# Two chained transformer blocks on one core: projections with 512 weight columns moving over 128 stationary tokens

## The chip, the core and the metric

The kernel runs on one core of a Trainium2 chip. The metric is the device time of one launch in microseconds; the median of three runs is compared. Inputs and output lie in the chip's memory in float32; all weights (about 277 MB) are read once per launch.

## The reference, cut to what matters

256 tokens of width 1024 pass through two models of two layers each, one after the other. Each layer has a mixer and one or two feed-forward blocks of width 2816, six of them in all; two have a causal convolution of three taps on the gate:

```python
def conv_ffn(h, w_up, conv_w, conv_b, w_down):          # blocks 0 and 1
    u, g = jnp.split(h @ w_up, 2, axis=-1)
    g = causal_dwconv(g, conv_w, conv_b)
    return (jax.nn.silu(g) * u) @ w_down
def _swiglu(x, wg, wu, wd):                             # blocks 2 to 5
    return (jax.nn.silu(x @ wg) * (x @ wu)) @ wd
# first model:  x = x + f(rmsnorm(x)), a final rmsnorm at its end
# second model: x = x + s * rmsnorm(f(rmsnorm(x)))      # s = 0.5 or 1, a norm on the output too
```

The mixers, in order: an mLSTM with four heads of 192 ("a") beside attention to 256 memory tokens; attention in a band with a relative bias ("band", 12 heads) beside memory attention; a convolution module of 31 taps on 512 channels beside windowed attention ("swa", 8 heads); attention with forget gates ("fox", 16 heads). Each has an input projection from width 1024 and an output projection back to it.

## The kernel before

It is written engine by engine, with semaphores by hand. Matrix products run in float32r with each operand as a rounded high part and the rest: `three` (L1571) issues hi x hi, hi x lo and lo x hi. Every product of weights is thus three matmuls.

**Weights.** They come in 260 slots of 1 MB, SLOTW = 8 x 256 columns per partition, a ring of RING = 3. SyncE's `load` (L407) waits for lo_done of the slot three before and issues one DMA into raw. ScalarE's `split_hi` (L587) rounds raw into w_hi once PE has used that slot three before (w_used), VectorE's `split_lo` (L950) subtracts into w_lo. raw, w_hi and w_lo are three separate rings.

**Form.** x is kept with its features on the partitions (xT, 8 chunks of 128 by 256 tokens). `feature_major` (L1604) holds 128x128 blocks of weights stationary and moves 256 tokens:

```python
for m in range(widths):
    for k in range(NCH):
        ins = three(bank[:, m * SEQ:(m + 1) * SEQ], weights(base, k * COLS + m * P), source(k),
                    start=k == 0, stop=k == NCH - 1)
```

`token_major` (L1615), for values, holds 128 tokens stationary and moves the 256 columns of a slot; it is the smaller part. `down` (L1627) adds the two hidden chunks of a step into the eight chunks of the output, which stay in four banks acc.

**Feed-forward.** `ffn` exists on each engine (SyncE L429, ScalarE L638, VectorE L1018, PE L1688). A block has 11 steps of three slots (gate, up, down) of 48 matmuls each. PE runs, in a hardware loop, gate and up of step i and then down of step i-1, so the elementwise work of a step is beneath the next one's products. Gate and up are scaled by the norm's factor as they are taken from the banks (L1030, L1048), silu is ScalarE's (L662), the product L1054, its two parts L666 and L1058; with the convolution, L655 and L1039 add the taps.

**Norms.** ScalarE applies the gain to x (`apply_hi`, L610) and squares it; the sum over features crosses partitions, so PE does it: `light_mean` (L1656: L1659, L1660) on sums made by VectorE (L982, L983), and `square_mean` (L1640: 32 matmuls of one column at L1645, then L1652 to spread the factor) for the norms on outputs. `token_rstd` (L1662, L1666) brings the factor to the tokens' side. `first_slot` (L1670: L1677, L1678, L1682) orders the first slot's products by what is ready. `post` (L1001) updates x (L1007, L1008). Clears of acc are matmuls with zeros (L1698).

**Order around mixers.** `slot` and `project` (L1848, L1726) interleave projections with attention stages `scores`, `turns` (transposing the probabilities, L1800) and `values`. The 31 taps of two convolution channels are diagonal matmuls (L1984), those of the other two VectorE's (L1460). `narrow` (L1832) makes gate logits of 8 and 16 columns. At the end the output is transposed back (L2060) and stored.

## Time and profile before

| | us |
|---|---|
| median of 3 runs | 1859.78 |
| lowest and highest | 1851.17, 1880.07 |
| the profiled execution: span, first to last instruction | 1852.6 |

Of the profiled execution the span is what is shown; it lies between the lowest and the median run. Durations below come from it. A matmul's recorded length reaches into its successors, since matmuls are pipelined; what one costs in a dense stretch is the distance between two starts. Line numbers are those of the kernel above.

### The profile page before, as it was taken

Reading aid. Unit: us, or ns where it says so; the run is one execution under the profiler, and the core shown is the slowest. Engines: PE = TensorE matmul, PEld = TensorE weight load, DVE = VectorE, ACT = ScalarE, POOL = GpSimd, SP = SyncE. Lnnn points to the kernel's source line nnn. Section 1 sums busy time; section 2 is a strip of 40 time slices with the busy share of each in tenths; the row PEclk is TensorE's granted clock in tenths of the full one; section 3 lists DMA queues with packets and bytes.
Section 4 is the critical chain, followed back from the end, with each engine's and each line's share of the span. In section 5 each row is a group of like instructions: output and inputs, shape, how many; then the busy total and the mean of one; then the engine's idle time right before and its main releaser. Section 6 shows DMA issues by size and latency. Waiting matters only on the chain.

```text
span 1852.6 us, 33184 instructions
## 1 busy us (share of the span) xinstructions
PE 1768.5 (95%) x13819; PEld 1699.4 (92%) x13825; DVE 1124.6 (61%) x1411; ACT 806.7 (44%) x950; POOL 85.2 (5%) x120
## 2 busy tenths in 40 slices
PE   7998999999899999999998799998999899999998
PEld 7996999998599999999997789998999898889997
DVE  5864766675466666555578475556655644475554
ACT  4543544443454444433442553335434433444332
POOL 3000000000000000000086000000000000000000
PEclk9997999999899999999999899999999979899998
DMA  8441456574045554655522245553655432246551
GB/s 257 137 138 46 154 188 196 185 215 159 1 151 195 191 169 139 199 181 181 181 92 72 83 145 181 181 181 118 200 182 181 136 115 92 68 137 204 181 181 45
DMA packets 226905, 279.62 MB, mean 151 GB/s; under 512 B 6848, under 2 KB 208850, under 8 KB 226840
## 3 DMA queue, kind: packets, MB, share of 16 engines
q1 hardware_dynamic: 226200, 278.41, 46.6%
q8 instruction: 47, 0.77, 0.2%
q0 software_dynamic: 640, 0.29, 0.1%
q14 instruction: 18, 0.15, 0.0%
HBM read 277.48 MB, written 1.07 MB: 150 GB/s over the span
## 4 chain that ended last, share of the span: by engine, by line
PE 88%; DVE 8%; ACT 2%; DMA 1%; issue 1%; DVEq 0%; SPq 0%; ACTq 0%
PE two L1573 26%; PE two L1575 26%; PE two L1574 26%; PE two L1776 2%; PE two L1645 1%; DVE aux L1460 1%; DVE act_lo L972 1%; PE two L1800 1%; DVE xT L1008 1%; DVE qk L1007 1%; PE two L1782 1%; PE two L1926 1%; DMA raw<-in_w_kv 1%; PE two L1811 1%; PE two L1787 1%
## 5 line engine op out<-in xcount | busy, mean ns | idle before, releaser
L1573 PE MATMUL two<-act_hi,w_hi 128*128 128x256 f32 x2648 | 759.3, 287 | 11.7 <-DVE act_lo L1168 6.8
L1574 PE MATMUL two<-act_lo,w_hi 128*128 128x256 f32 x2648 | 754.4, 285 | 0.0
L1575 PE MATMUL two<-act_hi,w_lo 128*128 128x256 f32 x2648 | 754.4, 285 | 0.0
L956 DVE TENSOR_TENSOR w_lo<-raw,w_hi 128x2048 fp32r<-128x2048 f32 x260 | 595.7, 2291 | 251.9 <-ACT w_hi L596 251.3
L596 ACT CAST w_hi<-raw 128x2048 fp32r<-128x2048 f32 x260 | 494.9, 1903 | 375.2 <-PE two L1575 194.0
L1573 PEld LDWEIGHTS two<-act_hi,w_hi 128*128 128x128 f32 x2648 | 513.6, 194 | 15.2 <-DVE act_lo L1168 7.8
L1574 PEld LDWEIGHTS two<-act_lo,w_hi 128*128 128x128 f32 x2648 | 513.7, 194 | 0.3
L1575 PEld LDWEIGHTS two<-act_hi,w_lo 128*128 128x128 f32 x2648 | 513.4, 194 | 0.0
L1573 PE MATMUL two<-hid_hi,w_hi 128*128 128x256 f32 x1072 | 302.2, 282 | 8.6 <-DVE hid_lo L1058 8.6
L1575 PE MATMUL two<-hid_hi,w_lo 128*128 128x256 f32 x1072 | 301.6, 281 | 0.0
L1574 PE MATMUL two<-hid_lo,w_hi 128*128 128x256 f32 x1072 | 298.9, 279 | 0.0
L1573 PEld LDWEIGHTS two<-hid_hi,w_hi 128*128 128x128 f32 x1072 | 202.4, 189 | 9.8 <-DVE hid_lo L1058 9.8
L1574 PEld LDWEIGHTS two<-hid_lo,w_hi 128*128 128x128 f32 x1072 | 202.4, 189 | 0.0
L1575 PEld LDWEIGHTS two<-hid_hi,w_lo 128*128 128x128 f32 x1072 | 201.8, 188 | 0.0
L666 ACT CAST hid_hi<-work 128x512 fp32r<-128x512 f32 x66 | 40.9, 620 | 233.5 <-PE two L1575 222.8
L1058 DVE TENSOR_TENSOR hid_lo<-work,hid_hi 128x512 fp32r<-128x512 f32 x66 | 45.7, 692 | 121.7 <-ACT hid_hi L666 121.7
L1030 DVE TENSOR_TENSOR work<-two,rstd 128x512 f32<-128x512 f32 x66 | 45.6, 691 | 54.4 <-PE two L1575 54.1
L1677 PE MATMUL two<-act_hi,w_hi 128*128 128x256 f32 x176 | 49.7, 314 | 13.9 <-ACT act_hi L617 13.8
L655 ACT ACTIVATE work<-work,par 128x256 f32<-128x256 f32 x44 | 24.1, 595 | 89.4 <-DVE work L1030 89.4
L1573 PE MATMUL two<-w_hi,act_hi 128*128 128x256 f32 (+1 forms) x208 | 62.0, 298 | 0.0
L1574 PE MATMUL two<-w_lo,act_hi 128*128 128x256 f32 (+1 forms) x208 | 61.1, 294 | 0.0
L1575 PE MATMUL two<-w_hi,act_lo 128*128 128x256 f32 (+1 forms) x208 | 60.9, 293 | 0.0
(273 smaller groups left out, 1696.7 us busy)
## 6 DMA issues: line engine op xcount, KB each, us to landing
raw<-in_ffn_w_up SPq DMA_DIRECT2D x88, 1024.0 KB, 5.2
raw<-in_ffn_w_down SPq DMA_DIRECT2D x66, 1024.0 KB, 4.9
raw<-in_ffn_w_gate SPq DMA_DIRECT2D x44, 1024.0 KB, 5.3
raw<-in_a_w_in SPq DMA_DIRECT2D x13, 1024.0 KB, 5.2
raw<-in_fox_w_in SPq DMA_DIRECT2D x12, 1024.0 KB, 5.3
raw<-in_ab_w_in SPq DMA_DIRECT2D x7, 1024.0 KB, 5.3
raw<-in_w_kv SPq DMA_DIRECT2D x6, 1024.0 KB, 6.6
raw<-in_mem_w_kv SPq DMA_DIRECT2D x4, 1024.0 KB, 10.0
```

Source lines behind the costliest of these rows:

```text
L596: nc.scalar.copy(w_hi[:, r, :], raw[:, r, :]).then_inc(hi_done, 1)
L655: ins = nc.scalar.activation(gate_cv[:, j, :], gate_acc[:, j, :], ACT.Identity, bias=bb, scale=w2)
L666: nc.scalar.copy(hid_hi[:, :, :], hid[:, :, :]).then_inc(ff_hi, 1)
L956: nc.vector.tensor_tensor(w_lo[:, r, :], raw[:, r, :], w_hi[:, r, :], ALU.subtract).then_inc(lo_done, 1)
L972: nc.vector.scalar_tensor_tensor(out=act_lo[:, c, :], in0=xT[:, c, :], scalar=cols(col, c), in1=act_hi[:, c, :], op0=ALU.mult, op1=ALU.sub ...
L1030: nc.vector.tensor_tensor(gate_acc[:, :, :], pj[t % RING][:, :].rearrange("p (j t) -> p j t", j=2), rstd2, ALU.mult).then_inc(ff_raw, 1)
L1058: nc.vector.tensor_tensor(hid_lo[:, :, :], hid[:, :, :], hid_hi[:, :, :], ALU.subtract).then_inc(ff_lo, 1)
L1573: nc.tensor.matmul(dst, w[0], a[0], start=start, stop=False, skip_group_check=True)
L1574: nc.tensor.matmul(dst, w[0], a[1], start=False, stop=False, skip_group_check=True)
L1575: return nc.tensor.matmul(dst, w[1], a[0], start=False, stop=stop, skip_group_check=True)
L1677: nc.tensor.matmul(d, w[0], act_hi[:, k, :], start=k == 0 and m == 0, stop=False, skip_group_check=True)
L1776: ins = nc.tensor.matmul(dst[:, lo:hi], q[:, b * P:(b + 1) * P], k[:, 0:hi - lo], start=True, stop=kind not in ("fox", "band"), skip_group ...
```

## The change

Almost every function is rewritten. What it does:

- **Form.** In every projection the activations of 128 tokens (a block b, of two) are stationary, and 512 weight columns move. A group is 1024 x 512 weights: `project(name, b)` runs 24 matmuls for block 0 and, later, 24 for block 1. Gate and up of a step share a group (256 columns each); down and the output projections move 512 of the 1024 output columns.
- **Tokens.** x is kept with tokens on the partitions (x_tok). What needs features on the partitions is transposed by PE: x before each norm (16 of 128x128, `turn_x`), the hidden values (2 per block and step, 4 with the convolution), q, k, gates and keys (`turn`). Row sums come from ScalarE's accum_out, so the statistics on PE, `narrow` and the clears go; gate logits are columns of a group of 264.
- **Slots.** 520 slots of half a megabyte in a ring of 10. raw and w_lo are the same memory, so a slot is loaded again only when PE is done with the slot ten before (FREED). Gate and up come as two DMAs per slot. ScalarE and VectorE split up to a given slot at given places (`splits`).
- **Out of step.** Block 0 is finished before block 1 in the last step and in the output projections, so that its norm can start. The loops of the feed-forward blocks are written out.
- **Mixers.** band: the last two pairs' stages lie in the output projection. fox: pairs 0 to 2 between projections, 3 to 7 after them, one at a time. swa: 26 of VectorE's 62 taps before the keys are taken.

Its core, with the rest left out (in this order: buffers, SyncE's waits, the order of ScalarE in a block, `arrive` between blocks, ScalarE's and VectorE's part of a step without the convolution, PE's `project` and its feed-forward block; VectorE's order is ScalarE's):

```diff
-COLS = 256
-RING = 3
-SLOTW = NCH * COLS
+HALF = 512
+RING = 10
+SLOTE = 1056
...
-        raw = sb("raw", [P, RING, SLOTW])
-        w_hi = sb("w_hi", [P, RING, SLOTW], F32R)
-        w_lo = sb("w_lo", [P, RING, SLOTW], F32R)
-        xT = sb("xT", [P, NCH, SEQ])
+        w_hi = sb("w_hi", [P, RING, SLOTE], F32R)
+        with nc.sbuf_tensor("raw", [P, RING, SLOTE], F32) as raw:
+            pass
+        w_lo = sb("w_lo", [P, RING, SLOTE], F32R)
+        x_tok = sb("x_tok", [P, NTB, D])
...
+            def slot_free(t):
+                if t < RING:
+                    return
+                kind, n = FREED[t - RING]
+                sp.wait_ge({"tm": w_tm, "pj": pj_full[1], "dn": w_dn, "acc": acc_full}[kind], n)
...
+                for s in range(2, LAST):
+                    go(s, 0)
+                    splits(first + 6 * s + 7)
+                    out_of(s, 0)
+                    splits(first + 6 * s + 9)
+                    go(s, 1)
+                    splits(first + 6 * s + 11)
+                    out_of(s, 1)
+                    splits(first + 6 * s + 13)
...
+            def arrive(e, key, table):
+                first = OUT[EVENTS[e]][0] + NCH if EVENTS[e] in OUT else FFN_AT[EVENTS[e]] + 6 * STEPS
+                ni = NORMS[key][2]
+                fetch_table(ACT.Sqrt)
+                for b in range(NTB):
+                    if e >= POST:
+                        moment_h(e, b)
+                    if e == FINAL:
+                        moment_x(N_FINAL, b)
+                    if b:
+                        moment_x(ni, 0)
+                    normed_hi(key, b)
+                    if b == 0:
+                        splits(first + 3)
+                moment_x(ni, 1)
+                splits(first + 5)
...
+                def silu(s, b):
+                    nc.scalar.activation(gate_t[b], pj[b][:, 0:FW], ACT.Silu, scale=rx[:, b:b + 1]).then_inc(ff_ga[b], 1)
...
+                def gated(s, b):
+                    nc.vector.scalar_tensor_tensor(out=hid_t[b], in0=pj[b][:, FW:2 * FW], scalar=rx[:, b:b + 1], in1=gate_t[b],
+                                                   op0=ALU.mult, op1=ALU.mult).then_inc(pj_free[b], 1)
...
+            def project(name, b):
+                a, ns, n = GROUPS[name]
+                per = NCH // ns
+                if GI[name]:
+                    pe.wait_ge(pj_free[b], GI[name])
+                for k in range(NCH):
+                    t = a + k // per
+                    if k % per == 0:
+                        slot_ready(t)
+                    hi, lo = whole_slot(t, per)
+                    mm(pj[b][:, 0:n], act_part(0, k, b), hi[:, k % per, :], k == 0, False)
+                    mm(pj[b][:, 0:n], act_part(0, k, b), lo[:, k % per, :], False, False)
+                    ins = mm(pj[b][:, 0:n], act_part(1, k, b), hi[:, k % per, :], False, k == NCH - 1)
...
+                for s in range(2, LAST):
+                    project((f, s), 0)
+                    down(s - 1, 1, (0, 1))
+                    turn_hid(s, 0)
+                    project((f, s), 1)
+                    down(s, 0, (0, 1))
+                    turn_hid(s, 1)
+                project((f, LAST), 0)
+                down(LAST - 1, 1, (0,))
+                turn_hid(LAST, 0)
+                project((f, LAST), 1)
+                down(LAST, 0, (0,))
+                turn_hid(LAST, 1)
+                down(LAST, 0, (1,))
+                down(LAST - 1, 1, (1,))
+                down(LAST, 1, (0, 1))
```

With the convolution, `take` (ScalarE) brings gate and up out of the bank, PE turns all four chunks, and `conv_hid` runs over ScalarE and VectorE by turns: copy into a padded buffer, six operations on 128 columns (one per tap and chunk), silu, product, high part, low part.

## Rows read from the trace of the kernel before

**Rows 1.** The page: its first line, part 1, and PEclk of part 2

```profile
span 1852.6 us, 33184 instructions
PE 1768.5 (95%) x13819; PEld 1699.4 (92%) x13825; DVE 1124.6 (61%) x1411; ACT 806.7 (44%) x950; POOL 85.2 (5%) x120
...
PEclk9997999999899999999999899999999979899998
```

**Rows 2.** The page, part 4: the chain that ended last, by engine

```profile
PE 88%; DVE 8%; ACT 2%; DMA 1%; issue 1%; DVEq 0%; SPq 0%; ACTq 0%
```

**Rows 3.** Stretches: PE, PEld, DVE, ACT, POOL busy us, PEclk, DMA share, GB/s

```profile
588.82:605.99 17.17, 17.17 (x147) 17.17 (x145) 11.18 (x12) 7.87 (x7) 0.00 (x0) 1.00 0.54 183
...
1332.00:1349.17 17.17, 17.17 (x146) 17.17 (x145) 9.65 (x7) 6.77 (x5) 0.00 (x0) 1.00 0.58 183
1250.29:1297.65 47.36, 41.71 (x333) 39.84 (x333) 32.66 (x42) 25.02 (x31) 0.00 (x0) 1.00 0.39 123
...
1835.00:1852.60 17.60, 10.89 (x73) 9.16 (x71) 8.04 (x15) 4.07 (x8) 0.00 (x0) 0.73 0.16 60
```

**Rows 4.** PE in order of time: start us, us; feed-forward, narrow, half clock

```profile
1320.25 0.28 PE L1574 MATMUL two<-hid_lo,w_hi 128*128 128x256 f32 x1
1320.37 0.28 PE L1575 MATMUL two<-hid_hi,w_lo 128*128 128x256 f32 x1
...
80.53 0.25 PE L1575 MATMUL two<-gw_hi,act_lo 128*128 128x8 f32 x1
80.64 0.25 PE L1573 MATMUL two<-gw_hi,act_hi 128*128 128x8 f32 x1
...
1473.02 0.41 PE L1677 MATMUL two<-act_hi,w_hi 128*128 128x256 f32 x1
1473.23 0.41 PE L1678 MATMUL two<-act_hi,w_lo 128*128 128x256 f32 x1
```

**Rows 5.** L1984 alone in 10 us: PE and PEld busy, PEclk, DMA

```profile
978.00:988.00 10.00, 10.00 (x48) 8.73 (x47) 1.00 0.94 296
```

**Rows 6.** PE by line: form, count | busy us, mean ns | idle before

```profile
L1645 PE MATMUL two<-mean_w,nrm 128*128 128x1 f32 x224 | 26.3, 245 | 0.2 <-ACT nrm L636 0.2
L1800 PE MATMUL two<-ident,p_sb 128*128 128x128 f32 x140 | 22.6, 307 | 17.6 <-DVE p_sb L1161 17.6
...
L1659 PE MATMUL two<-nrm,mean_w 128*128 128x256 f32 x20 | 7.0, 431 | 6.2 <-DVE nrm L983 6.1
...
L1698 PE MATMUL two<-zero 128*128 128x512 bf16 x18 | 5.5, 422 | 0.5 <-issue 0.2
```

**Rows 7.** In order of time, PE, a turn of eight

```profile
493.50 1.09 PE L1800 MATMUL two<-ident,p_sb 128*128 128x128 f32 x8 [2.27 <-DVE p_sb L1161]
```

**Rows 8.** VectorE and ScalarE by line: form, count | busy us, mean ns

```profile
L1039 DVE SCALAR_TENSOR_TENSOR work<-work,par 128x255 f32<-128x255 f32 x44 | 19.4, 481 | 32.8 <-ACT work L655 32.8
...
L982 DVE TENSOR_TENSOR nrm<-nrm 128x1024 f32<-128x1024 f32 x10 | 12.3, 1230 | 5.4 <-ACT nrm L622 5.4
...
L1161 DVE TENSOR_SCALAR p_sb<-p_sb,small 128x128 f32<-128x128 f32 x36 | 10.2, 284 | 0.6
...
L596 ACT CAST w_hi<-raw 128x2048 fp32r<-128x2048 f32 x260 | 494.9, 1903 | 375.2 <-PE two L1575 194.0
...
L666 ACT CAST hid_hi<-work 128x512 fp32r<-128x512 f32 x66 | 40.9, 620 | 233.5 <-PE two L1575 222.8
```

**Rows 9.** The page, part 6: KB each, us from issue to landing

```profile
raw<-in_ffn_w_gate SPq DMA_DIRECT2D x44, 1024.0 KB, 5.3
...
out_x<-qk SPq DMA_DIRECT2D x4, 256.0 KB, 2.0
```

**Rows 10.** In order of time, PE: turns of two successive pairs of band

```profile
472.62 0.82 PE L1800 MATMUL two<-ident,p_sb 128*128 128x128 f32 x6
...
478.25 0.82 PE L1800 MATMUL two<-ident,p_sb 128*128 128x128 f32 x6
```

**Rows 11.** The chain in order of time: VectorE's taps in the swa mixer

```profile
978.33 16.65 DVE aux L1460 x41
```

More of the change, by code:

```diff
@@ L685, in projection @@
-            def projection(first, n, take=None, after=None, ahead=()):
-                for t in range(first, first + n):
-                    if t - first not in ahead:
-                        split_hi(t + 2)
-                    if take:
-                        take(t, t - first)
-                    if after and t - first in after:
-                        after[t - first]()
-            def out_projection(first):
-                for j in range(4):
-                    split_hi(first + j + 2)
-                    post_squares(j, first + 3, None)
+            split = [0]
@@ L760, in _ @@
[L760 to L774 removed]
+            act.wait_ge(ident_ready, 1)
@@ new lines, in _ @@
+            for j in range(3):
+                for b in range(NTB):
+                    take_kv(j, b)
+                    if j == 2:
+                        normed_hi("band", b)
+                    splits(GROUPS[f"KV{j}"][0] + 9 + 2 * b)
+            for j in range(2):
+                for b in range(NTB):
+                    to_tk(f"BIN{j}", "band", b).then_inc(pj_free[b], 1)
+                    splits(GROUPS[f"BIN{j}"][0] + 9 + 2 * b)
+            attention("band", lambda n: splits(137) if n == 1 else None)
@@ new lines, in _ @@
+            exps("fox", 1)
+            take_pair(2, 1)
+            o_hi("fox", 0)
+            pt_copy("fox", 1)
+            take_pair(3, 0)
+            o_hi("fox", 1)
+            exps("fox", 2)
+            take_pair(3, 1)
+            pt_copy("fox", 2)
+            for n in range(3, 8):
+                exps("fox", n)
+                o_hi("fox", n - 1)
+                pt_copy("fox", n)
+            o_hi("fox", 7)
+            splits(459)
+            arrive(EV["fox"], 5, ACT.Silu)
+            ffn(5, False)
@@ L939, in _ @@
+            fetch_table(ACT.Sqrt)
+            for b in range(NTB):
+                moment_h(EV[5], b)
         @block.vector
@@ L1569, in _ @@
+            o_lo("fox", 7)
+            splits(459)
+            arrive(EV["fox"], 5)
+            ffn(5, False)
+            for b in range(NTB):
+                residual(EV[5], b)
         @block.tensor
         def _(pe):
[L1571 to L1575 removed]
@@ new lines, in _ @@
+            for b in range(NTB):
+                pe.wait_ge(al, 8 * b + 8)
+                project("M0", b)
+            pe.wait_ge(params_in, 16 * 16)
+            for n in range(PARAM_TILES):
+                ins = nc.tensor.transpose(acc[1][n // 4][:, n % 4 * P:(n % 4 + 1) * P], prow[:, n, :], ident[:, :])
+                if n in (3, 4):
+                    ins.then_inc(par_ps, 1)
+            turn("M0", 0, 2)
+            project("M1", 0)
+            turn("M0", 1, 2)
+            turn_x("a", 0)
@@ new lines, in attention_start, with pair_ready @@
+            def attention_start(phase):
+                last = len(PAIRS[phase])
+                for n in range(last):
+                    scores(phase, n)
+                    if n >= 1:
+                        turns(phase, n - 1)
+                    if n >= 2:
+                        values(phase, n - 2)
+            def pair_ready(phase, first):
+                return lambda c, b: pe.wait_ge(h_olo, PAIR0[phase] + c - first + 1)
+            attention_start("band")
+            pe.wait_ge(h_olo, PAIR0["band"] + 6)
@@ new lines, in _ @@
+            scores("fox", 0)
+            project("FP2", 0)
+            turn("FP1", 1, 4)
+            turns("fox", 0)
+            scores("fox", 1)
+            project("FP2", 1)
+            turn("FP2", 0, 4)
+            values("fox", 0)
+            turns("fox", 1)
+            project("FP3", 0)
+            turn("FP2", 1, 4)
+            values("fox", 1)
+            scores("fox", 2)
+            project("FP3", 1)
+            turn("FP3", 0, 4)
+            turns("fox", 2)
+            scores("fox", 3)
@@ new lines, in _, with last_turns, last_values @@
+            turn("FP3", 1, 4)
+            values("fox", 2)
+            all_taken("FP3", "FP3")
+            for n in range(3, 7):
+                turns("fox", n)
+                scores("fox", n + 1)
+                values("fox", n)
+            pe.wait_ge(h_olo, PAIR0["fox"] + 6)
+            def last_turns():
+                turns("fox", 7)
+            def last_values():
+                values("fox", 7)
+            project_out("fox", pair_ready("fox", 0), {1: last_turns, 3: last_values})
```

2179 lines of the change are left out of this document (1140 added, 1039 removed).

## The prediction

> **What bounds the kernel now.** I read the page from its top. TensorE is busy 95% of the span, VectorE 61%, ScalarE 44%, and the strip of 40 slices shows PE at 9 nearly everywhere at a granted clock of 0.9 to 1.0 [rows 1]. A busy PE need not be one that sets the end, so the chain of waits comes next: 88% of it is PE, 8% DVE, 1% DMA [rows 2]. Then the six feed-forward blocks by stretch: a step of one takes 17.17 us, with the convolution or without, PE busy in all of it, VectorE 9.6 to 11.2, ScalarE 6.8 to 7.9, at full clock [rows 3]. A step has three slots of 48 matmuls, 144, so one costs 17.17/144 = 119.2 ns. There are 260 slots: 12,480 such matmuls, 1488 us of 1852.6. The rest (365 us) is attention, convolution, mLSTM, statistics and what PE waits. So the price of one matmul is the question.
>
> **What one matmul costs.** All are 128x128 weights under 256 moving columns, and start 120 ns apart (the last of a feed-forward slot 120 or less) [rows 4]. Two rows bracket what that is. The narrow products with only 8 moving columns still start 110 ns apart (80.53, 80.64): that is the weight load's pace. And where the granted clock was 0.5 (1.2 GHz), the same 256-column form starts 213 ns apart, 256/1.2, with a new weight block each time: with 213 ns of streaming the load is hidden whole [rows 4]. The taps L1984 say the same at full clock: 10 us hold 48 of them, one or two of which are cut by the edges, so they start 208 to 217 ns apart, each with its own weights [rows 5]. At full clock the 256 columns themselves would need 107 ns, less than the load, so today the load sets the pace and the columns are nearly free.
>
> **Part 1, 512 columns over one load.** The columns in all stay the same and the loads halve. New count: 87 groups of 48 with 512 columns (4176), 66 down steps of 24 (1584), four output projections of 96 (384), 6144 in all, and four narrow groups (256 or 264 columns) of 48, 192. The form isn't in the trace. Its floor is 213 ns (a column per cycle at 2.4 GHz, from the 213 at half that clock), its ceiling two of today's, 238. I take 216, the 213 of streaming and a little, which lies in L1984's 208 to 217. Then 6144 x 0.216 + 192 x 0.12 = 1350 us against 1488: **-138**. At 213 it is -156, at 238 -3.
>
> **Part 2, tokens on the partitions need turning.** Added transpositions of 128x128: hidden values 4 per plain step and 8 per step with convolution (352), x ten times 16 less today's 16 (144), q, k, gates and keys 114, less the 16 at the end: 594. Eight of L1800 take 1.09 us, one 0.31, so (1.09-0.31)/7 = 0.11 apart [rows 7]: **+65**. Bounds: 0.11, and 0.307 if each took its whole length (+182). In the Trainium skill, "TensorE: Matmul & The Clock Gate", Part 4 (PE-mode transpose), such a transposition took about 275 ns in one kernel's context; by it the sum here would be 163 us instead of 65. The trace disagrees for groups of them, which is how the change issues them; I stay with the row.
>
> **Part 3, statistics leave PE.** Row sums come from ScalarE's accumulator. Gone: L1645 (26.3 us), L1659 and its twin L1660 (7.0 and somewhat less, 13), L1652 and L1666 (44 at 0.11: 5), the narrow products (96 x 0.11, partly at half clock: 14), the clears L1698 (5.5) [rows 6]: **-64**. Parts 1 to 3 are all on PE and so on the path: -138 +65 -64 = -137.
>
> **Part 4, does a step keep up?** A plain step on PE: 72 x 0.216 + 4 x 0.11 = 16.0 us; with convolution 16.4. Splitting half a megabyte: ScalarE between 620 ns (512 columns, L666) and 1903 (2048, L596), by the line through them 1.05 us; VectorE 1.23 (L982 has that size) [rows 8]. Six of each are 6.3 and 7.4 us, plus some 2 each for silu, products and parts: no bound. What can bind is the order. raw and w_lo are now one buffer, so a load waits for PE's last use ten slots before, no longer for the split three slots before. Call the start of project(s, 0) zero. Slots 6s+8 and 6s+9 come free at 7.1 and 7.8, in down(s-1, 1). 1 MB lands in 5.3 us and 256 KB in 2.0 [rows 9]; the second of two half-megabytes so lands about 5.2 after the first's issue, at 12.5. Cast 13.6, silu(s, 1) 14.1 (its project ended at 13.2), VectorE's split 14.8, gated product 15.3; turn_hid(s, 1) is due at 15.7. It holds by 0.4 us. All other slots have over 3 us. With the convolution ScalarE and VectorE pass the block to and fro five times. For block 0 that is about 4.6 us beneath 5.2 of matmuls. For block 1 the splits of 6s+10 and 6s+11 stand before it on VectorE, conv_hid starts some 1.5 us late (six operations of 128 columns, between the 284 ns of L1161 and the 440 of L1039: about 2 us), and down(s, 1) waits about 1 us. Queued behind it are hi and lo of the next slots, which have slack. I take 1.0 us x 22 steps: **+22** (bounds 0 and 2 per step). SP issues 10 loads a step at 0.37 us where it had 3; it waits for slots most of the time, so nothing. The loops are written out, so code is fetched where it was repeated; straight stretches today run at the same 120 ns: nothing.
>
> **Part 5, the joints.** From the last steady step to the first of the next block takes 47.36 us where two steps take 34.34 [rows 3]: 13.0 for a joint with a norm on the output, of which 5 are PE's statistics (32 L1645 at 0.11, a few more). After: block 0's sums and update (squares of 512 columns as L666, 0.6 twice, small ones, two updates on VectorE of 0.7, between L1039 and L982: about 4.2 us) lie under 3.9 us of block 1's down products; then 16 turns (1.8). But ScalarE does normed_hi of block 0 and two splits (4.5 us) before block 1's squares, so PE runs dry after block 0's first 16 products, about 4 us. 1.8+0.5+4 = 6.3. For six such joints -6.5 each; statistics and turns of these are in parts 2 and 3, so what is new here is small: the idle time stays about as it was. I take 0. The end: 17.6 us from the statistics to the last store, with four transposed stores; about 7 after, of it -4 not counted yet.
>
> **Part 6, the rest.** Memory keys start when half a megabyte is there: -6. band: the last two pairs of eight lie under the output projection; a pair comes every 5.63 us [rows 10]: -5. swa: the taps stood alone on the chain for 16.65 us [rows 11]; 26 of 62 now lie beneath projections: -10. fox: pairs 3 to 7 come after the projections one at a time (about 9 us each, half of it PE), where only two did: +7. Sum: -18, with the end.
>
> **Sum.** -137 +22 +0 -18 = -133: 1852.6 - 133 = 1720 us by the profiled span, which has nothing beside it but the start of the launch. The median of the runs shown is 1859.8, 0.4% above it, so 1720 x 1.004 = **1726 us**.
>
> **Rivals.** (A) The 120 ns are 107 of streaming plus 13 of changing weights, whatever the width: 226 ns, 6144 x 0.010 = +61, **1787**. For it: 120 is above both the load's pace and the streaming. Against: 213 at half clock and 217 at L1984 leave no room. (B, the slower side) **The slot chain sets the step.** If the second half-megabyte lands later than 5.6 us after the first's issue, turn_hid(s, 1) waits, every wait delays the slots' release, and nothing catches up; the two engines' strict order adds the convolution's. The gate and up slots are two loads each of 256 KB; if none overlapped, eight at 2.0 us and two at 3.1 would make a step of 22 us, and midway between that and my 16.3 lies 19.2: 66 x 2.9 = +191, **1917**. It decides against the change once the mean step is over 18.3, 2.0 above mine. For it: 0.4 us of slack, and three times as many loads. Against: the DMA engines are 0.55 busy in a step [rows 3], and a late block has slack elsewhere. A weaker form (0.7 us a step) gives 1772. (C) Each turn takes its whole 0.307, as a mean L1800 does [rows 6], where it stands between other matmuls: 594 x 0.20 = +119, **1845**. For it: here they come in twos and fours, not eights. Against: nothing waits between them. The figure of the Trainium skill's Part 4 above points the same way. (D) No stall in the convolution and block 1's joint hidden: -22 -15, **1689**. (E) The new order hides nothing and the form costs 238: +135, 1861; the rows on 213 and 217 leave it almost nothing.
>
> **How the numbers follow.** Chances: forecast 0.54, A 0.10, B 0.06, its weak form 0.13, C 0.04, D 0.12, E 0.01. Forecast 1726; the range takes in D's, A's and the weak B's spread, from 1665 to 1800. This kernel's measurement tells about 2% from no change, so the bounds are 1823 and 1897 us: faster takes the forecast, D, the weak form and nearly all of A, 0.87; same takes C, E and the edges, 0.08; slower is what of B exceeds 2% and unforeseen waits of that kind, 0.05.
>
> **What would show it.** Right: in the timeline w_hi matmuls of 512 columns start 215 to 217 ns apart (A: 226; E: 238); a plain step lasts 16.0 us, one with convolution 17.4; transpositions 0.11 apart; PE's idle time before its turns of hidden values and its down products about 1 us per convolution step and next to none in a plain one; in the joints one wait of about 4 us before the second turning of x. Wrong: idle time of PE released by w_lo in the middle of blocks (B), or a granted clock that falls in the joints.

## The result and the profile after

The changed kernel takes 1914.47 us (median of 4 runs, 1909.69 to 1915.55) against 1869.92 of the runs of before beside it; without the disturbed ones the ratio is 1.031, 95% interval 1.028 to 1.034. It is 3% slower where 7% faster was forecast. The profiled execution has a span of 1913.8, 61.2 more than before's 1852.6. Its page, the rows that answer to [rows 1, 2] (first line, part 1, PEclk of part 2, engines of part 4) and three groups of part 5:

```profile
span 1913.8 us, 20929 instructions
PE 1770.6 (93%) x7823; PEld 1393.0 (73%) x7823; DVE 1059.2 (55%) x1848; ACT 934.2 (49%) x1599; POOL 82.3 (4%) x128
...
PEclk9997999999799999999998899999999998589999
...
PE 71%; DVE 11%; DMA 7%; ACT 6%; SPq 3%; issue 1%; DVEq 0%; ACTq 0%
...
L1704 PE MATMUL two<-w_hi,act_parts 128*128 128x512 f32 (+2 forms) x3120 | 1021.2, 400 | 38.0 <-DVE w_lo L1138 24.3
...
L647 ACT CAST w_hi<-raw 128x1024 fp32r<-128x1024 f32 (+1 forms) x520 | 533.9, 1053 | 203.4 <-DMA raw<-in_ffn_w_up 159.2
```

Two things stand in it. PE's matmuls are nearly halved in number (7823 records for 13819), yet PE is busy for the same time, 1770.6 us for 1768.5. And the chain is no longer PE's alone: 71% for 88%, the rest VectorE, DMA, ScalarE and SyncE's queue, so waits of another kind have come. ScalarE's casts now wait 159 us for loads of w_up; that alone would cost nothing, if the casts were early enough.

The strip shows one new place, a 5 in slice 35 of PEclk (1627 to 1675 us), in the fox mixer.

Stretches of after (us, then PE, PEld, DVE, ACT, POOL busy, PEclk, DMA share, GB/s): a plain step, a later plain step, one with convolution, step 3 of the first block, and fox's pairs after the last projection. Before had 17.17 for every step [rows 3].

```profile
1172.76:1189.81 17.05, 17.05 (x78) 13.86 (x77) 8.89 (x10) 7.82 (x10) 0.00 (x0) 1.00 0.55 185
1189.81:1207.78 17.97, 17.27 (x78) 13.79 (x77) 8.87 (x10) 7.79 (x10) 0.00 (x0) 1.00 0.54 175
628.17:645.94 17.77, 17.77 (x81) 14.23 (x80) 12.54 (x22) 9.47 (x14) 0.00 (x0) 1.00 0.54 178
246.12:269.33 23.21, 18.15 (x81) 14.01 (x80) 12.01 (x22) 9.76 (x14) 1.41 (x2) 1.00 0.95 280
...
1625.00:1690.00 65.00, 50.94 (x161) 32.51 (x162) 17.99 (x84) 14.59 (x50) 0.00 (x0) 0.50 0.02 6
```

A plain step in which PE never waits takes 17.05 us, not the 16.0 of the forecast: that is the form's price. The next one takes 0.9 more and PE is busy for 0.7 less than the stretch: that is a wait. The form's pace is seen in order of time (PE, start us, us); the starts lie 0.22 to 0.24 apart, where [rows 4] had 0.12 for half the columns:

```profile
1175.75 0.39 PE L1704 MATMUL two<-w_hi,act_parts 128*128 128x512 f32 x1
1175.98 0.39 PE L1704 MATMUL two<-w_lo,act_parts 128*128 128x512 f32 x1
1176.21 0.62 PE L1704 MATMUL two<-w_hi,act_parts 128*128 128x512 f32 x2
1176.66 0.39 PE L1704 MATMUL two<-w_lo,act_parts 128*128 128x512 f32 x1
```

**A ledger of PE.** All of PE's intervals from one start to the next, added up by what started them; what goes beyond 245 ns (512 weight columns), 135 (fewer weight columns, and the sums L1645, L1659, L1660), 115 (the new turnings) or 700 (all else) is counted as waiting. So the last row also has some products that ran at half clock, and the attention row some short waits.

```
us                                     before    after   difference   forecast
products of weights                    1497.8   1447.6      -50        -138
turnings to the features' side            1.7     56.3      +55         +65
statistics on PE, with the clears        56.1      0        -56         -64
products of attention and the rest      179.3    211.2      +32        }  +4
waiting                                 108.2    188.7      +80        }
sum                                      1843     1904      +61        -133
```

The miss is 194 us: 88 in the pace of the products, 108 in waits and in attention and the rest, 8 in the statistics, and 10 the other way in the turnings. The experiments take the first two in turn.

One stage has over half of the 61 us. From its first products to those of the next stage the fox mixer takes 170.4 us before and 204.9 after, at a mean granted clock of 0.87 and 0.77 (before from L1677 to L1677, after from one turning of x to the next):

```profile
1472.50:1642.90 170.40, 167.23 (x1111) 149.26 (x1113) 86.13 (x192) 67.33 (x123) 0.00 (x0) 0.87 0.31 100
...
1507.30:1712.20 204.90, 175.04 (x729) 131.80 (x728) 83.67 (x212) 82.51 (x170) 0.53 (x1) 0.77 0.29 96
```

### The profile page after: what moved, and what is told of

It is laid out like the page before. It is cut to its first block, busy times and chain, and to the rows that moved or that the text cites. A ratio compares the mean times of both kernels' runs of the same rounds, so it can differ in the third digit from the quotient of the medians.

```text
span 1913.8 us, 20929 instructions
## 1 busy us (share of the span) xinstructions
PE 1770.6 (93%) x7823; PEld 1393.0 (73%) x7823; DVE 1059.2 (55%) x1848; ACT 934.2 (49%) x1599; POOL 82.3 (4%) x128
## 4 chain that ended last, share of the span: by engine, by line
PE 71%; DVE 11%; DMA 7%; ACT 6%; SPq 3%; issue 1%; DVEq 0%; ACTq 0%
PE two L1704 59%; DMA raw<-in_ffn_w_up 6%; DVE w_lo L1138 4%; ACT w_hi L647 3%; PE two L1762 2%; PE two L1895 2%; DMA raw<-in_ffn_w_down 2%; SPq L451 1%; PE two L1918 1%; PE two L2143 1%; PE two L1900 1%; SPq L452 1%; ACT act_parts L686 1%; PE two L1776 1%; DVE act_parts L1155 1%
## 5 line engine op out<-in xcount | busy, mean ns | idle before, releaser
L1704 PE MATMUL two<-w_hi,act_parts 128*128 128x512 f32 (+2 forms) x3120 | 1021.2, 400 | 38.0 <-DVE w_lo L1138 24.3
L1138 DVE TENSOR_TENSOR w_lo<-raw,w_hi 128x1024 fp32r<-128x1024 f32 (+1 forms) x520 | 623.5, 1223 | 265.8 <-ACT w_hi L647 261.4
L1704 PEld LDWEIGHTS two<-w_hi,act_parts 128*128 128x128 f32 x3120 | 593.3, 192 | 173.6 <-DVE w_lo L1138 27.1
L647 ACT CAST w_hi<-raw 128x1024 fp32r<-128x1024 f32 (+1 forms) x520 | 533.9, 1053 | 203.4 <-DMA raw<-in_ffn_w_up 159.2
L1704 PE MATMUL two<-w_lo,act_parts 128*128 128x512 f32 (+1 forms) x1560 | 612.0, 393 | 0.0
L1704 PE MATMUL two<-w_hi,hid_parts 128*128 128x512 f32 x1008 | 337.9, 396 | 5.6 <-DVE hid_parts L1244 5.4
L1704 PEld LDWEIGHTS two<-w_lo,act_parts 128*128 128x128 f32 x1560 | 300.3, 192 | 58.4
L1704 PEld LDWEIGHTS two<-w_hi,hid_parts 128*128 128x128 f32 x1008 | 189.4, 188 | 54.8 <-DVE hid_parts L1244 11.8
L1704 PE MATMUL two<-w_lo,hid_parts 128*128 128x512 f32 x504 | 198.1, 393 | 0.0
L1704 PEld LDWEIGHTS two<-w_lo,hid_parts 128*128 128x128 f32 x504 | 94.7, 188 | 21.1
L724 ACT ACTIVATE p_sb<-two,rx 128x256 f32<-128x256 f32 x88 | 41.6, 472 | 117.4 <-PE two L1704 117.4
```

What stands on the lines that cost most here:

```text
L647: nc.scalar.copy(w_hi[:, t % RING, 0:n], raw[:, t % RING, 0:n]).then_inc(hi_done, 1)
L724: nc.scalar.activation(gate_t[b], pj[b][:, 0:FW], ACT.Silu, scale=rx[:, b:b + 1]).then_inc(ff_ga[b], 1)
L1138: nc.vector.tensor_tensor(w_lo[:, r, 0:n], raw[:, r, 0:n], w_hi[:, r, 0:n], ALU.subtract).then_inc(lo_done, 1)
L1704: return nc.tensor.matmul(dst, a, w, start=start, stop=stop, skip_group_check=True)
```

## Experiments on the price of the form

**forms.** Matmuls alone, 96 of a form in a row, on tiles made ready before (float32r if not said otherwise).

```diff
+            run(512)      # 2 the form of the change
+            run(256)      # 3
+            run(384)      # 4
+            run(128)      # 5
+            run(512, wide=64)      # 11 64 stationary columns
+            run(512, rows=64)      # 12
+            mm(bank[3][:, 0:SEQ], plain[:, 0:P], plain[:, 256:512], i == 0, i == 23)      # 13 plain float32
```

> A kernel of matmuls alone, 96 of each form in a row, copies x to the output and computes nothing of the reference. It measures what one matmul costs from start to start at full clock. Rows of the two traces: 256 columns 120 ns, 512 columns 231 ns; at half clock 213 and 426, so nothing beside the streaming there. Theory F (a fixed price for changing weights, none of it hidden): 384 columns 160+13 to 18 = 173 to 178 ns, 512 with 64 stationary columns the same 231, one weight block repeated 231. Theory L (the load of the next weights takes reads from the stream of 4-byte columns): 64 stationary columns about 222, 64 rows the same 231, bf16 213 at 512 columns since load and stream are half as large. Theory B (VectorE and ScalarE disturb the reads): 213 to 216 here with both idle, 231 only in the last group, where both are busy. My theory is L at 0.6, F at 0.3, B at 0.1. All: 128 columns 108 to 110.

Median interval between two starts of a group, and what is left when a column per cycle at 2.4 GHz is taken off:

```
128 columns              111 ns      -        bf16, 256 columns       109 ns    2
256                      120        13        bf16, 512               216       3
384                      173        13        64 stationary columns   230      17
512                      227        14        64 rows                 227      14
256 tokens over weights  120        13        plain float32, 256      216 and 213, two records each
```

Five stretches of it (10 us of 256 columns, of 512, of bf16 512, of 64 stationary columns, and of 512 beside busy VectorE and ScalarE; a window's count has one or two cut at its edges), at a granted clock of 1.00, the upper level:

```profile
58.00:68.00 10.00, 10.00 (x86) 10.00 (x85) 0.00 (x0) 0.00 (x0) 0.00 (x0) 1.00 0.01 2
...
110.00:120.00 10.00, 10.00 (x46) 8.29 (x45) 0.00 (x0) 0.00 (x0) 0.00 (x0) 1.00 0.00 0
152.00:162.00 10.00, 10.00 (x47) 4.55 (x47) 0.00 (x0) 0.00 (x0) 0.00 (x0) 1.00 0.00 0
...
184.00:194.00 10.00, 10.00 (x45) 5.85 (x44) 0.00 (x0) 0.00 (x0) 0.00 (x0) 1.00 0.01 2
...
258.00:268.00 10.00, 10.00 (x46) 8.29 (x45) 4.85 (x9) 2.92 (x6) 0.00 (x0) 1.00 0.00 0
```

The 13 ns are fixed: the same at 256, 384 and 512 columns, whichever operand is held. That is rival A of the prediction, which I had given 0.10. My own theory of this experiment fell: 64 stationary columns, whose load is shorter (5.85/44 = 133 ns for 184), save nothing. One weight block repeated, four banks in turn and busy neighbours change nothing either (227 each). bf16 pays 3 ns, which agrees with the formula of the Trainium skill, "TensorE: Matmul & The Clock Gate", Part 2 (back-to-back issue gap): N/2.4 GHz and about 2.5 ns. The 131 ns at 512 columns which the same section gives for a sustained stream is not what these rows show (216). The float32r form pays some 10 ns more than bf16. The cause inside PE stays open. Plain float32 shows where the forecast went wrong: its 256 columns are two records of 213 to 216 ns each, so each passes at two cycles of 2.4 GHz per column, and so do the taps of [rows 5] (62 products, 124 records).

**halves.** The kernel after with each product of 512 columns as two of 256. Both halves of a first product carry the start flag into one bank, and the output is not the reference's; the products and columns that pass through PE are those of a correct split.

```diff
+                if n == 512:
+                    nc.tensor.matmul(dst[:, 0:256], a, w[:, 0:256], start=start, ...)
+                    return nc.tensor.matmul(dst[:, 256:512], a, w[:, 256:512], start=start, ...)
```

> The kernel after with each matmul of 512 columns issued as two of 256 over the same tokens; everything else stays. It gives what the wide form is worth in this kernel. If the wide form costs 231 and the narrow one 120, 6144 x 9 ns = 55 us more than after, 1970 us less what idle time absorbs (some 90 us of waits, of which those for PE's own work stay): 1955 to 1970. If the wide form were free streaming at 213 (the forecast), the narrow would cost 150 us more, 2065. If the slots and not PE set the time of a step (rival B of the prediction), nothing changes: 1914 to 1925.

1945.45 us, ratio 1.052 (1.045 to 1.059) to before: 2.1% over after's 1.031, some 39 us, and less than the 1955 to 1970 expected. A pair of halves takes 239.2 ns on average from start to start, the whole 230.8, so 6144 x 8.4 = 52 us of PE, of which the waits take a part. The wide form is a gain, but of 8 ns, not of 22.

**forms2.** In forms the product takes 227, in after 231, in a pattern (224 to 238) that comes back in every step. This run issues the steps of after without anything else.

```diff
+            for g in range(4):      # 2 slots 1024 apart
+                project(4 * g, 1024, b4[0:2], act)
+            for g in range(4):      # 3 slots 1056 apart, as in the kernel
+                project(4 * g, 1056, b4[0:2], act)
```

> A kernel of matmuls alone that copies x to the output and computes nothing of the reference: the project and down products of the kernel after, 4 steps of each kind. The form alone took 227 ns in the first kernel of matmuls, the kernel after has a mean of 231, in a pattern of 224 to 238 that repeats from step to step whatever VectorE and ScalarE do. Theory A (the place of the slots in memory, 1056 columns apart instead of 1024): 227 with slots 1024 apart, 231 with 1056. Theory W (waits and marks of semaphores): 227 without, 231 with them. Theory T (the products for down and the turns between them): 227 until these come in. If all stay at 227, what PE reads is not the cause, and how it gets its instructions is what is left.

Mean interval: 226.7 ns with slots 1024 columns apart, 230.5 with 1056, 226.9 with 1088; waits, marks, down products and turns add nothing (230.5 to 230.6). 40 us at 1024, at 1056 and at 1088:

```profile
52.00:92.00 40.00, 40.00 (x178) 33.15 (x177) 0.00 (x0) 0.00 (x0) 0.00 (x0) 1.00 0.00 0
96.00:136.00 40.00, 40.00 (x176) 32.57 (x175) 0.00 (x0) 0.00 (x0) 0.00 (x0) 1.00 0.00 0
...
300.00:340.00 40.00, 40.00 (x179) 33.11 (x178) 0.00 (x0) 0.00 (x0) 0.00 (x0) 1.00 0.00 1
```

So the slots' place costs 4 ns per product on average. 1056 columns are 16.5 times 256 bytes, so every other slot starts in the middle of such a block; 1024 and 1088 are whole multiples. Three distances were tried; that the 256 bytes are what counts is read from these alone.

**align.**

```diff
-SLOTE = 1056
+SLOTE = 1088
```

> The kernel after with slots 1088 columns apart (17 x 256 bytes) instead of 1056 (16.5 x 256), one constant. In the second kernel of matmuls slots 1024 or 1088 apart gave 226.8 ns between starts, 1056 gave 230.5. If that is so here, 6144 matmuls become 3.7 ns shorter: 23 us of PE's time; with what the waits take of it 12 to 23 us less than the kernel after on this chip. If the waits for slots are the bound, PE waits longer by what it saves: 0 to 8 us.

1911.17, where the kernel after on the same chip took 1919.01 (**after_again**, below): 8 us, which is within what one kernel moves between chips. The median interval falls to 227, but that into the turnings rises from 374 to 421 ns on average (158 of them): PE waits where it had worked.

**twice.** sched (below) with each turning of hidden values issued twice.

```diff
-                for c in range(n):
+                for c in list(range(n)) * (1 if isinstance(name, str) else 2):
```

> sched with each turning of hidden values issued twice (352 more of 128x128, the second writes what the first wrote); otherwise the result is the same. In sched nothing waits in the steps: 17.03 us plain, 17.51 with convolution. If a turning costs its distance in a dense group (109 ns, part 2 of the prediction), a plain step lasts 17.03 + 4 x 0.109 = 17.47, one with convolution 17.51 + 8 x 0.109 = 18.38, and the whole is 38 us over sched: 1935. If each cost its whole recorded length (0.28, rival C), 18.15 and 19.75 and 98 us more, 1995.

1927.05, 29 us over sched (on another chip). The steps, where nothing else is idle, are exact: a plain one 17.50 for 17.04, one with convolution 18.36 for 17.51.

```profile
1178.57:1196.07 17.50, 17.50 (x82) 14.30 (x81) 8.72 (x11) 7.37 (x10) 0.00 (x0) 1.00 0.54 180
646.64:665.00 18.36, 18.36 (x90) 15.19 (x89) 12.45 (x23) 9.43 (x15) 0.00 (x0) 1.00 0.52 173
```

0.46/4 and 0.85/8: 0.11 us each. Rival C is dead, and part 2 stands. The 275 ns that the Trainium skill's "TensorE: Matmul & The Clock Gate", Part 4 (PE-mode transpose) gives for a transposition is close to the recorded length here (273 ns on average in sched), not what one costs in a group.

## Experiments on the waits

What happens in the slow step of after: the chain in order of time from 1189.30, when PE is done with a slot of down.

```profile
1189.31 0.37 SPq L451
...
1189.72 1.20 SPq L452
...
1190.97 0.47 SPq L451
...
1191.48 4.93 DMA raw<-in_ffn_w_up
...
1196.43 1.06 ACT w_hi L647
...
1197.52 1.22 DVE w_lo L1138
1198.74 0.41 DVE p_sb L1217
...
1199.19 0.44 PE two L1762 x2
```

The block's silu (L724) could start at 1195.9 but stands behind the cast of slot 6s+9 on ScalarE, whose load has just landed; the gated product stands behind the split on VectorE; the turning is 0.70 us late. This is the place and the order of the prediction's part 4, which found 0.4 us of slack: it let 4.7 us pass from the release to the landing, and 7.1 pass (1189.30 to 1196.41), since SyncE's issues take 0.4 to 1.2 us each where four are due at once, and 256 KB land in 4.9, not 2.0. The row of 2.0 was a store's [rows 9]; the loads of 256 KB here take 4.0 to 4.7 by the medians of the page.

**sched.** The splits of 6s+8 and 6s+9 behind block 1's silu and product.

```diff
                     out_of(s, 0)
-                    splits(first + 6 * s + 9)
                     go(s, 1)
-                    splits(first + 6 * s + 11)
+                    splits(first + 6 * s + 9)
                     out_of(s, 1)
-                    splits(first + 6 * s + 13)
+                    splits(first + 6 * s + 11)
```

> The kernel after with ScalarE's and VectorE's splits of slots 6s+8 and 6s+9 behind silu and product of block 1 instead of ahead of them, and the later ones one place later too (in the steps 2 to 9 of a block). In after 158 waits ahead of a turning of hidden values cost 23 us above the pace of the products, and the chain of waits names loads of w_up there. If those are this order (rival B, weak form: ScalarE stands waiting for a slot that was released in the middle of the step while block 1's silu is due), 12 to 20 us less than after, the plain steps at 17.05 us all. If the loads are late wherever the splits stand, the wait moves to w_lo in the products: within 5 us of after.

1897.57 against 1919.01: 21 us, ratio to before 1.024 (1.022 to 1.027). The same steps as above (ahead: plain, plain, convolution):

```profile
1172.88:1189.92 17.04, 17.04 (x77) 13.87 (x76) 8.71 (x11) 7.38 (x10) 0.00 (x0) 1.00 0.56 186
1189.92:1206.97 17.05, 17.05 (x78) 13.87 (x77) 8.73 (x11) 7.38 (x10) 0.00 (x0) 1.00 0.57 185
636.38:653.89 17.51, 17.51 (x82) 14.30 (x81) 12.27 (x23) 9.33 (x15) 0.00 (x0) 1.00 0.56 181
```

From the third step of a block on, all but one of them are now at PE's own pace (one, beside the band's table, took 22.4). The loads were in time for the products; only silu behind them was not. It also shows that the convolution stalls nothing: 17.51 is 17.04 and four more turnings.

**after_again** is the kernel after on the chip of align, sched and fox_warm.

> The kernel after itself, unchanged, on the chip of this call, so that the others are read against it: 1.031 times before, 1907 to 1915 us where before is 1850.

1919.01, ratio 1.038 (1.035 to 1.040). The first runs gave 1.031: the kernel moves by half a per cent and more between chips, or with where its clock falls, and smaller differences between chips are read as nothing.

**align_sched.** 

> align and sched together: slots 1088 columns apart and the splits behind block 1's silu. align alone gave 8 us, sched alone 21, against the kernel after on the same chip (1919). If align's missing 15 us went into waits for slots (its mean interval into the turnings grew from 374 to 421 ns while the products' median fell from 231 to 227), the two together give more than their sum: 40 to 46 us, 1873 to 1879, a plain step of 72 x 0.2268 + 0.43 = 16.76 us. If the waits come back once PE is faster, about 29 us, 1890.

1896.64, ratio 1.024 (1.018 to 1.029): the steps take 16.87 (plain) and 17.28 where sched had 17.04 and 17.51, and the total is within the spread of sched's. Of the two sums expected, 40 to 46 and 29 us, the smaller is the nearer: 22 measured, 26 by the ratios.

**joint** and **joint2.** The ten joints between blocks. In after PE waits at four of them for the split of the third slot, and at five for x ahead of a turning. This one has both (PE in order of time; idle 1.92 and 0.86, from start to start 2.3 and 1.3):

```profile
974.74 0.40 PE L1704 MATMUL two<-w_lo,act_parts 128*128 128x512 f32 x1
977.06 0.50 PE L1704 MATMUL two<-w_hi,act_parts 128*128 128x512 f32 x1 [1.92 <-DVE w_lo L1138]
...
980.25 1.32 PE L1776 MATMUL two<-ident,x_tok 128*128 128x128 f32 x8 [0.86 <-DVE x_tok L1179]
```

```diff
                     if b:
                         moment_x(ni, 0)
+                    else:
+                        splits(first + 3)
                     normed_hi(key, b)
-                    if b == 0:
-                        splits(first + 3)
```

Besides this, both halves of down(LAST-1, 1) stand together in the last step.

> The kernel after with two moves at the ten joints: in the last step both halves of down(LAST-1, 1) stand together, so that its two slots are released some 8 us earlier, and the splits up to first+3 stand before the first high parts of the next norm instead of behind them. If the 2.3 us in which PE waits for a w_lo in the first products of each block and the 1.3 us before the second turning of x come from the late release and the splits' place, 6 to 9 joints give back 2 to 3.5 us each: 13 to 30 us less, about 1893. If the chain of sums and x's update sets the joint anyway, within 5 us of 1914.

1913.28, ratio 1.034 (1.031 to 1.037), no change: at the same joint the waits (1.90 and 0.85 us) are there as before, now both ahead of x.

> The kernel after with the early release of two slots of joint, and in each joint the sums and the update of x of both blocks ahead of the high and low parts of the next norm, with the splits between block 0's and block 1's. In joint the waits stayed 2.3 and 1.3 us and only changed places, since ScalarE and VectorE had the same work ahead of the second turning of x. If their order is the bound, x of block 1 is ready some 4 us earlier, PE's first products start about 1.5 us later, and the ten joints give back 1 to 2.5 us each: 1890 to 1904. If the amount of their work is the bound (some 13 us of ScalarE in 14 us), within 4 us of 1914.

1930.08, ratio 1.044 (1.038 to 1.049), slower than any expectation. Its steps had more waits of sched's kind (up to 18.5 us), and band ran 65 us at half clock (24 in after). Two orders of the same work have not shortened the joints; that the amount of ScalarE's and VectorE's work is their bound fits this and isn't shown. Why joint2 is slower rather than the same isn't separated from the waits and the clock.

**relb.** The band's table in six pieces. In after the whole of it stands ahead of the weights of step 4: the stretch from 246.12 above, DMA share 0.95.

```diff
-            ffn(0, ..., {4: load_relb})
+            ffn(0, ..., {s: (lambda s=s: load_relb(s - 4)) for s in range(4, 10)})
```

> The kernel after with the band's table of biases (2.3 MB in rows of 512 and 1024 bytes) loaded in six pairs of DMAs ahead of steps 4 to 9 of the first feed-forward block instead of two DMAs ahead of step 4. Steps 3 and 4 of that block take 23.2 and 19.1 us where the others take 17.7. If that is the table standing ahead of the weights on SyncE's queue while the ring holds under two steps, 5 to 6 us less: about 1908. If the whole table costs its bytes anyway, no change, 1914.

1912.21, ratio 1.034 (1.031 to 1.037). That step falls from 23.21 to 18.77 us, the total can't be told from after. The row of the step:

```profile
240.74:259.51 18.77, 17.98 (x82) 14.15 (x80) 12.45 (x22) 9.26 (x14) 0.00 (x0) 1.00 0.64 189
```

**fox.** The scores of the next pair but one ahead of the values of this one (ScalarE's and VectorE's parts moved likewise).

```diff
+            scores("fox", 4)
             for n in range(3, 7):
                 turns("fox", n)
-                scores("fox", n + 1)
+                if n < 6:
+                    scores("fox", n + 2)
                 values("fox", n)
```

> The kernel after with the scores of fox's pairs 4 to 7 issued one pair earlier on PE and VectorE and ScalarE's exponentials one pair earlier, so that two pairs are under way after the projections. If the 12.6 us per pair are the chain PE, VectorE, ScalarE, VectorE, PE of one pair at a time, at half clock because PE idles 3.6 us in each, four pairs fall to 6 to 8 us each and the clock rises: 18 to 26 us less, about 1892. If the two engines' work per pair (about 4.5 us each) or the half clock stays the bound, 5 to 10 us less, about 1906.

1909.16, ratio 1.033 (1.028 to 1.038), in the whole no difference from after's 1.031. PE's turnings of successive pairs start 12.6 us apart in after, 10.6 in fox, with 3.2 and 1.1 us of waiting ahead of them. Both at half clock:

```profile
1640.05 1.51 PE L1918 MATMUL two<-ident,p_sb 128*128 128x128 f32 x6 [3.11 <-DVE p_sb L1332]
1652.61 1.54 PE L1918 MATMUL two<-ident,p_sb 128*128 128x128 f32 x6 [3.16 <-DVE p_sb L1332]
```

and fox, the same, then its stretch:

```profile
1653.86 1.54 PE L1921 MATMUL two<-ident,p_sb 128*128 128x128 f32 x6 [1.13 <-DVE p_sb L1334]
1664.41 1.54 PE L1921 MATMUL two<-ident,p_sb 128*128 128x128 f32 x6 [1.13 <-DVE p_sb L1334]
...
1622.00:1683.00 61.00, 52.31 (x164) 33.43 (x165) 19.02 (x85) 14.69 (x50) 0.00 (x0) 0.50 0.02 6
```

**fox2.** Pairs 0 to 4 between the projections.

> The kernel after with fox's pairs started one group earlier: pairs 0 to 4 between the projections, pairs 5, 6 and 7 after them with two under way. The first fox kernel took the waits away (3.6 to 1.6 us per pair) and gained 5 us only, because the granted clock stayed at 0.5 for 61 us, as long as no projection stood between the stages. If that stretch at half clock is what fox costs, it shrinks to some 20 us here, and the time falls by 25 to 30 us to about 1887. If the price is the pairs' own work on the three engines (12 us per pair wherever it stands), no more than 5 to 8 us are gained, about 1907.

1936.72, ratio 1.045 (1.042 to 1.049). The mixer takes 206.7 us, in after 204.8: nothing gained, and the half clock only moved; 82 us of it between 1550 and 1720, where after had 89.

**fox_warm.** fox with products that nobody reads.

```diff
+                if phase == "fox" and n >= 3:
+                    pe.wait_ge(h_max, g + 1)
+                    for _ in range(8):
+                        nc.tensor.matmul(place[g][:, 0:512], warm[:, 0:P], warm[:, :], start=True, stop=True, ...)
                 pe.wait_ge(h_p, g + 1)
```

> The kernel fox (two pairs under way) with eight bf16 products of 512 columns, whose results nobody reads, ahead of the turnings of pairs 3 to 7, where PE waits for the probabilities. fox2 showed that moving pairs ahead of projections gains nothing, so either the clock or the pairs' work is what fox costs. If the granted clock follows how busy PE is, the 61 us at 0.5 shrink to under 20 us and the stretch after the last projection falls from 10.5 us per pair to 7 or 8, 10 to 15 us less than fox, about 1895. If the clock stays at 0.5, the eight products add 8 x 0.427 = 3.4 us to each of five pairs, less the 1.6 us idle: 9 us more than fox, 1918.

1898.27, ratio 1.026 (1.023 to 1.028): 21 us under after on the same chip, and 11 under fox. Pairs are now 7.1 to 9.5 us apart, and the stretch that had 0.50:

```profile
1621.00:1686.00 65.00, 60.68 (x251) 37.80 (x255) 20.82 (x87) 17.86 (x56) 0.00 (x0) 0.76 0.10 33
...
1652.95 0.82 PE L1927 MATMUL two<-ident,p_sb 128*128 128x128 f32 x6
1660.05 0.87 PE L1927 MATMUL two<-ident,p_sb 128*128 128x128 f32 x6
```

Work added to PE makes PE faster: in after it is busy 50.9 of 65 us and its clock stays at 1.2 GHz, here it is busy 60.7 and at 2.4 for about half of the stretch; a turning of six takes 0.82 instead of 1.5. The stretch at half clock was expected under 20 us and is 31. The Trainium skill, "TensorE: Matmul & The Clock Gate", Part 1 (what's actually happening), says that the throttled clock is the default and that activity releases it; these rows agree.

Not all of the 21 us is made there. From its first turning of probabilities to the next turning of x the mixer takes 129.9 us in after (129 to 131 in eight more kernels with the same order, 134.9 in after_again), 123.7 in fox and 118.4 in fox_warm: 6 us from the order and 5 from the unread products. Ahead of that turning, where no edit reaches, executions differ by up to 5 us (70.9 in fox, 75.0 in fox_warm), and the band mixer was 5 us shorter than in after_again.

**best1** and **best2.** All of align, sched, fox, the unread products and relb; best2 with such products in band.

> align, sched, fox, warm (the eight unread products ahead of fox's turnings, from a bf16 column read with stride 0) and relb together. What they gave alone, against after: 8 to 23, 21, 21 (fox and warm), 2 to 5. If they lie on different parts of the path, as I hold, 1919 less 60 to 70: about 1853, level with before (1850). If part of the gain is the same idle time twice, 1870.

1870.54 (7 runs), ratio 1.009 (1.005 to 1.013): the second of the two expectations, in which part of the gain is the same idle time twice.

> best1 with four unread products ahead of the turnings of band's pairs 0 to 5 as well. In six runs of kernels with the same band the clock there was at 0.5 for 10, 14, 24, 24, 34 or 55 us, and the stage took up to 10 us more where it was 55. If more work on PE keeps the clock up there as in fox, the half-clock stretch stays under 14 us and the stage at 141 us from the second turning of x to the next; the products cost 6 x 0.85 us where PE is the bound: between 3 us less and 3 us more than best1, with less spread. If the clock falls anyway, they cost 6 x 1.7 = 10 us.

1875.67, ratio 1.011 (1.004 to 1.018), so nothing more is gained. The parts give back two thirds and more of what was lost, and the kernel is still 0.9% slower than before. No version here beats it.

## Why the prediction was wrong

Two steps failed, part 1 and part 6, and in part 4 a term was too small.

- **What bounds the kernel, and the counts: right.** PE's products set the time, their number and that of the turnings came as counted.
- **Part 1, the form: the first step that failed.** "I take 216, the 213 of streaming and a little, which lies in L1984's 208 to 217." In the kernel it is 231: -50 us instead of -138. The 13 ns above the streaming were in [rows 4] (120 for 107), and I laid them to the load's pace of 110. The two rows that were to show that a longer stream hides them are both of a column per two cycles of 2.4 GHz, one by the clock, one by plain float32 (forms). At a column per cycle they stay, at any width. 4 ns more are the slots' place (forms2), which nothing in the trace of before could show. The rival with this mechanism (A, 226) was the better reading; its 1787 us was still far from 1914, since the rest of the miss lies elsewhere.
- **Part 2, turnings, 0.11 each: right** (twice; +55 in the ledger, and some 10 more in the first products behind them, 314 ns to the next start for 231).
- **Part 3, statistics: right.** 56 us where 64 were forecast.
- **Part 4, does a step keep up: the order was right, a term mis-sized.** The landing took 7.1 us from the release and not 4.7, which made 0.4 us of slack a wait in part of the steps: rival B's weak form, 21 us of the total (sched). Its strong form, the slots as the bound of each step, did not come. The 22 us for the convolution came to nothing (17.51, exact).
- **Part 5, joints: near in size, not in place.** The joint shown waits 2.8 us, in two places, where 4 were forecast in one; the others range from nothing to 5 us ahead of a turning of x.
- **Part 6, fox: the second step that failed, "one at a time (about 9 us each)".** They came 12.6 us apart. Two pairs under way make it 10.6 (fox), unread products beside them 8.3 on average (fox_warm). What the 9 left out is first of all the granted clock, 0.50 for 65 us; one pair at a time at full clock was not run. The mixer went from 170.4 to 204.9 us, +34 where +7 was forecast. fox_warm gives 11.5 of these back; the other 23 stay open.
- **The arithmetic of it.** The form's true gain (-50) is eaten by its own turnings (+55). What is left is the -56 of the statistics, and the waits (+80) with the dearer rest (+32) turn that into +61. Of the waits, 21 us are the splits' order (sched); joint, joint2, relb and fox, one by one, gained nothing that stands out of the kernel's own spread.

## What to carry to other kernels

Before widening a matmul's moving side, compare intervals between starts at the same type and the same columns per cycle: a row that is slow for another reason (half clock, plain float32) hides every fixed price. Count the transpositions that the new layout needs against that gain first; here they alone exceeded it. Where an engine's order is written by hand, put work that waits for a load behind the work that the busiest engine waits for, and look up the granted clock of an attention stage before its price is taken from rows at full clock.

## What was not expected of the hardware

- A float32r product pays about 13 ns over its columns at full clock, bf16 3, and neither pays at half clock (float32r 213 ns for 256 columns in before and 427 for 512 in after; bf16 427 for 512 in fox_warm).
- With every other slot of moving rows starting 128 bytes off a multiple of 256, 512 columns take 4 ns more on average (230.5 for 226.8, forms2).
- Eight unread bf16 products ahead of each of five turnings made the stretch that holds them 5 us shorter (123.7 us in fox, 118.4 in fox_warm; the whole kernels 1.033 and 1.026 of before).
- The band mixer, untouched by them, ran from 17 to 65 us at half clock in different kernels (17 in fox_warm, 65 in sched, align, joint and joint2), and its stage (from one turning of x to the next) took 159 to 163 us where it was 65 and 149.5 in after; what decides it stays open.
